# Sums of squares of a hybrid decoder layer as two rounded products, with their low parts on GpSimd

## The reference

```python
def _rms_norm(x, g, eps):
    y = xf * lax.rsqrt(jnp.mean(xf * xf, axis=-1, keepdims=True) + eps)
    return (y * g.astype(jnp.float32)).astype(x.dtype)

q = _rms_norm(q.reshape(b, s, ATTN_HEADS, 2, ATTN_HEAD_DIM), q_g, RMS_EPS) * (ATTN_HEAD_DIM ** -0.5)
k = _rms_norm(k.reshape(b, s, ATTN_HEADS, 2, ATTN_HEAD_DIM), k_g, RMS_EPS)
...
o = _rms_norm(o, sub_g, RMS_EPS) * (1.0 - lambda_init)
```

## Time and profile before

| | us |
|---|---|
| median of 3 runs | 1872.85 (1872.35 to 1877.61) |
| the profiled execution | 1872.82 |
| its span | 1870.8 |
| busy TensorE | 1827.9 |
| busy VectorE | 1133.2 |
| busy ScalarE | 942.4 |
| busy GpSimd | 359.4 |

### The profile page before, as it was taken

How to read it: one execution, slowest core, us unless ns; L and a number is a source line. 1 busy time by engine, 2 the same in 40 slices (tenths; PEclk the granted TensorE clock), 3 DMA queues, 4 the chain that set the end, 5 groups by cost and what they waited for, 6 DMA issues and landing times.

```text
span 1870.8 us, 27353 instructions
## 1 busy us (share of the span) xinstructions
PE 1827.9 (98%) x8653; PEld 1298.2 (69%) x8653; DVE 1133.2 (61%) x1373; ACT 942.4 (50%) x1310; POOL 359.4 (19%) x401
## 2 busy tenths in 40 slices
PE   8999999999999999999999999999999999999997
PEld 6887887887888888887655565566556655665553
DVE  7867867867867333458664565456545654565456
ACT  5676676666667222325454455445544554455441
POOL 1322332332330000013021112111211121112010
PEclk9999999999999999999999999999999999999999
DMA  5232232232241222458999999999999999999998
GB/s 203 86 124 93 80 132 92 78 128 102 79 138 57 94 97 98 162 197 318 421 421 421 421 422 421 422 421 422 421 422 421 421 421 422 421 422 421 422 420 335
DMA packets 95377, 520.06 MB, mean 278 GB/s; under 512 B 13522, under 2 KB 20858, under 8 KB 45032
## 3 DMA queue, kind: packets, MB, share of 16 engines
q1 hardware_dynamic: 87672, 501.08, 67.2%
q0 software_dynamic: 6944, 16.30, 2.2%
q10 hardware_dynamic: 720, 2.16, 0.3%
HBM read 511.52 MB, written 25.51 MB: 287 GB/s over the span
## 4 chain that ended last, share of the span: by engine, by line
PE 81%; DMA 10%; DVE 5%; issue 2%; ACT 1%; DVEq 0%; SPq 0%; ACTq 0%
PE bank L1924 18%; PE bank L1300 15%; PE bank L1682 10%; DMA big<-in_w 10%; PE bank L1955 7%; PE bank L1330 7%; PE bank L1964 6%; PE bank L1729 2%; DVE w_lo L2520 2%; PE bank L1947 2%; PE bank L1375 2%; PE bank L1358 1%; PE bank L1867 1%; DVE x_lo L2532 1%; PE bank L1442 1%
## 5 line engine op out<-in xcount | busy, mean ns | idle before, releaser
L2520 DVE TENSOR_TENSOR w_lo<-big,w_hi 128x2048 fp32r<-128x2048 f32 x141 | 321.9, 2292 | 204.6 <-ACT w_hi L2211 204.6
L2211 ACT ACTIVATE w_hi<-big 128x2048 fp32r<-128x2048 f32 x141 | 268.8, 1918 | 231.1 <-DMA big<-in_w 203.1
L1955 PE MATMUL bank<-big,keep 128*64 128x512 f32 x896 | 203.3, 598 | 0.0
L2520 DVE TENSOR_TENSOR w_lo<-keep,w_hi 128x2048 fp32r<-128x2048 f32 x48 | 109.9, 2292 | 104.0 <-ACT w_hi L2211 103.6
L1300 PE MATMUL bank<-h_hi,wm_hi 128*128 128x512 f32 x408 | 168.8, 414 | 0.0
L1300 PE MATMUL bank<-h_hi,wm_lo 128*128 128x512 f32 x408 | 159.7, 391 | 0.0
L1300 PE MATMUL bank<-h_lo,wm_hi 128*128 128x512 f32 x408 | 159.1, 390 | 0.0
L2211 ACT ACTIVATE w_hi<-keep 128x2048 fp32r<-128x2048 f32 x48 | 92.2, 1921 | 107.3 <-DMA keep<-in_w 97.6
L1955 PEld LDWEIGHTS bank<-big,keep 128*64 128x64 f32 x896 | 59.9, 136 | 117.3 <-issue 117.2
L1924 PE MATMUL bank<-w_hi,x_hi 128*128 128x512 f32 x480 | 134.5, 402 | 3.8 <-DVE w_lo L2520 3.8
L1924 PE MATMUL bank<-w_lo,x_hi 128*128 128x512 f32 x480 | 129.0, 391 | 0.0
(11 more groups left out here) (398 smaller groups left out, 3628.3 us busy)
## 6 DMA issues: line engine op xcount, KB each, us to landing
big<-in_w SPq DMA_DIRECT2D x290, 1024.0 KB, 13.4
keep<-in_w SPq DMA_DIRECT2D x94, 1024.0 KB, 14.2
big<-in_w_mix SPq DMA_DIRECT2D x72, 512.0 KB, 3.3
keep<-in_w_tail SPq DMA_DIRECT2D x44, 512.0 KB, 3.3
keep<-in_x SPq DMA_DIRECT2D x8, 512.0 KB, 4.5
aux<-acum_rows SPq DMA_DIRECT2D x16, 256.0 KB, 3.7
big<-acum_rows SPq DMA_DIRECT2D x16, 256.0 KB, 3.5
keep<-y_tok SPq DMA_DIRECT2D x4, 1024.0 KB, 13.1
```

Source lines behind the costliest of these rows:

```text
L1955: ins = pe.matmul(bank[2 * (c // 2)][r, :], x_s[:, n % 4, CS * (n // 4):CS * (n // 4 + 1)], raw[s][:, c * 512:(c + 1) * 512], start=False, ...
L2211: act.activation(w_hi[:, s], raw[r], ACT.Copy).then_inc(hi_ready, 1)
L2520: dve.tensor_tensor(w_lo[:, s], raw[r], w_hi[:, s].bitcast(F32), ALU.subtract).then_inc(lo_ready, 1)
```

## The change

The three sums of a step become two rounded products each: the block of ones by the high part of the squares (rounded to float32r) and by the low part (square minus high part), added up in PSUM. The ones are copied once to float32r (`block_r`, `ones_r`); for the third sum the stationary operand is one column broadcast to 128.

- ScalarE gets three copies a step: `high_square(0)` and `high_square(1)`, each behind a `take_xb`, and one behind the square of the output. They write to the place of the logits. `make_decay(1)` moves ahead of `root(0)`.
- GpSimd gets three subtractions a step (`low_square`), two behind `make_xs(0)` and one at the end of the step, where the mask of the next step's first chunk moves ahead of it; the mask of its second chunk is behind it. Its last step is written out like those of the other engines.
- TensorE: `project_vz(0)` is cut in three. Its first two blocks of weights run before `y_and_state(0)`; three follow `turn_xb(2)`; then comes `sum_squares(0)`, then the last three, then `sum_squares(1)`. A part of the projection now waits only for the pieces of the value weights that it reads. The third sum moves one quarter of projection 3 further back, and each sum waits for its low part.
- Two semaphores of the routing are taken over from others.

```diff
+        block_r, ones_r = parts("block_r", [P, P], big_base, loop_mem.at + 4 * D), sb("ones_r", [P, 1], F32R)
+        sq_hi, sq_lo = parts("sq_hi", [P, 2, T], aux_base, 0), parts("sq_lo", [P, 2, T], keep_base, 23552 - 3 * KT * P)
...
+                def low_square(i, n, at):
+
+                    pool.wait_ge(sqhi_ready.sem, sqhi_ready.at(i, at))
+                    pool.tensor_tensor(sq_lo[:, n], sq[:, n], sq_hi[:, n].bitcast(F32), ALU.subtract).then_inc(
+                        sqlo_ready.sem, 1)
+
+                def body(i, more):
+                    make_seg(i, 1)
+                    make_xs(i, 0)
+                    low_square(i, 0, 1)
+                    low_square(i, 1, 2)
+                    make_seg(i, 2)
+                    make_xs(i, 1)
+                    make_seg(i, 3)
+                    make_xs(i, 2)
+                    make_xs(i, 3)
+                    if more:
+                        make_seg(i + 1, 0)
+                    low_square(i, 0, 3)
...
+                    def high_square(n):
+
+                        act.wait_ge(proj_read.sem, proj_read.at(i, n + 1))
+                        act.wait_ge(diff_ready.sem, diff_ready.at(i, 0))
+                        act.activation(sq_hi[:, n], sq[:, n], ACT.Copy).then_inc(sqhi_ready.sem, 1)
...
                     squares(0)
                     take_xb(0)
+                    high_square(0)
                     split(i, 7)
                     split(i, 8)
                     squares(1)
                     take_xb(1)
+                    high_square(1)
                     take_xb(2)
+                    make_decay(1)
                     root(0)
-                    make_decay(1)
...
                     act.activation(sq[:, 0], m1_b[:], ACT.Square).then_inc(osq_ready.sem, 1)
+                    act.wait_ge(osq_ready.sem, osq_ready.at(i, 1))
+                    act.activation(sq_hi[:, 0], sq[:, 0], ACT.Copy).then_inc(sqhi_ready.sem, 1)
...
-                    def project_vz(t):
-                        free_proj(i, 6 + t)
-                        pe.wait_ge(plo_ready.sem, plo_ready.at(i, PIECES))
+                    def project_vz(t, k0=0, k1=KT):
+                        if k0 == 0:
+                            free_proj(i, 6 + t)
+                        pe.wait_ge(plo_ready.sem, plo_ready.at(i, 6 + -(-k1 * VZ // D)))
...
-                        pe.matmul(s_b[n][:], block_ones, sq[:, n], start=True, stop=True).then_inc(sums_ready.sem, 1)
+                        pe.wait_ge(sqlo_ready.sem, sqlo_ready.at(i, n + 1))
+                        pe.matmul(s_b[n][:], block_r[:], sq_hi[:, n], start=True, stop=False)
+                        pe.matmul(s_b[n][:], block_r[:], sq_lo[:, n], start=False, stop=True).then_inc(
+                            sums_ready.sem, 1)
...
-                    sum_squares(0)
+                    project_vz(0, 0, KT // 4)
                     y_and_state(0)
                     turn_xb(2)
-                    project_vz(0)
+                    project_vz(0, KT // 4, 5 * KT // 8)
+                    sum_squares(0)
+                    project_vz(0, 5 * KT // 8, KT)
                     sum_squares(1)
...
                     turn_y(2, 8)
+                    project(i + 1, 3, KT // 2, 3 * KT // 4)
                     pe.wait_ge(osq_ready.sem, osq_ready.at(i, 1))
                     pe.wait_ge(logits_ready.sem, logits_ready.at(i, 4))
-                    pe.matmul(s_b[0][:], ones, sq[:, 0], start=True, stop=True).then_inc(osum_ready.sem, 1)
-                    project(i + 1, 3, KT // 2, KT)
+                    pe.wait_ge(sqlo_ready.sem, sqlo_ready.at(i, 3))
+                    pe.matmul(s_b[0][:], ones_r[:].to_broadcast([P, P]), sq_hi[:, 0], start=True, stop=False)
+                    pe.matmul(s_b[0][:], ones_r[:].to_broadcast([P, P]), sq_lo[:, 0], start=False, stop=True).then_inc(
+                        osum_ready.sem, 1)
+                    project(i + 1, 3, 3 * KT // 4, KT)
```

More of the change, by code:

```diff
@@ L633, in _ @@
             def _(pool):
[L634 removed]
+                prime(pool, seg_ready, sqlo_ready, xs_ready, gidx_ready, sidx_ready, pickb_ready, picks_ready, *spare_used[0:2])
                 pool.wait_ge(decays_ready, 3)
[L636 to L672 removed]
@@ new lines, in heads, with make_seg @@
+                def heads(table, i, u):
+                    return table[:, u, bass.ds(i * HPG, HPG)]
+                def make_seg(i, u):
+                    pool.wait_ge(rows_in[u % 2].sem, rows_in[u % 2].at(i, u // 2 + 1))
+                    of = seg_of[u % 2].rearrange("p k (h c) -> p k h c", h=2)
+                    at = heads(a_all, i, u).rearrange("p (k h) -> p k h", k=2)
+                    pool.tensor_tensor(of, of, at.unsqueeze(3).to_broadcast([P, 2, 2, P]), ALU.subtract).then_inc(
+                        seg_ready.sem, 1)
+                    pool.wait_ge(seg_ready.sem, seg_ready.at(i, 2 * u + 1))
+                    pool.tensor_tensor(of, of, tri.unsqueeze(1).unsqueeze(1).to_broadcast([P, 2, 2, P]), ALU.mult).then_inc(
+                        seg_ready.sem, 1)
@@ new lines, in make_xs @@
+                def make_xs(i, u):
+                    pool.wait_ge(m0_read.sem, m0_read.at(i, u + 1))
+                    pool.wait_ge(m1_ready.sem, m1_ready.at(i, min(2 * u, 6)))
+                    pool.wait_ge(ydiag_ready.sem, ydiag_ready.at(i, u))
+                    pool.wait_ge(y_read.sem, y_read.at(i, u))
+                    xv = xb[:, u, 0:GW].rearrange("p (h c) -> p h c", h=HPG)
+                    for dst, src in ((xdt, heads(dtv, i, u)), (xw, heads(wend, i, u))):
+                        pool.tensor_tensor(dst.rearrange("p (h c) -> p h c", h=HPG), xv,
+                                           bcast_inner(src, HD), ALU.mult)
+                    dsk = SMALL["d_skip"][0]
+                    pool.tensor_tensor(xd.rearrange("p (h c) -> p h c", h=HPG), xv,
+                                       bcast_inner(smalls[:, bass.ds(i * HPG + dsk, HPG)], HD),
+                                       ALU.mult).then_inc(xs_ready.sem, 1)
@@ L674, in _ @@
+                make_seg(0, 0)
+                pool.tensor_copy(block_r[:], block_ones)
+                pool.tensor_copy(ones_r[:], ones[:, 0:1])
+                steps_of_mixer(pool, body)
             @block.scalar
             def _(act):
-                prime(act, sigz_ready, phi_ready, ghi_ready, sigm_ready, mhi_ready, taps_ready, silu_ready, proj_read, root_ready, m0_read, decay_ready, exp_ready, yn_ready,
+                prime(act, sigz_ready, sqhi_ready, phi_ready, ghi_ready, sigm_ready, mhi_ready, taps_ready, silu_ready, proj_read, root_ready, m0_read, decay_ready, exp_ready, yn_ready,
@@ L1323, in body @@
                 def body(i, more):
-                    def project_vz(t):
-                        free_proj(i, 6 + t)
-                        pe.wait_ge(plo_ready.sem, plo_ready.at(i, PIECES))
+                    def project_vz(t, k0=0, k1=KT):
+                        if k0 == 0:
+                            free_proj(i, 6 + t)
+                        pe.wait_ge(plo_ready.sem, plo_ready.at(i, 6 + -(-k1 * VZ // D)))
                         hi, lo = (w[:].rearrange("p (a b) -> p a b", a=KT) for w in (vz_hi, vz_lo))
-                        for k in range(KT):
+                        for k in range(k0, k1):
                             for h, w in ((h_hi, hi), (h_hi, lo), (h_lo, hi)):
@@ L1332, in project_vz @@
                                                 stop=(k == KT - 1 and h is h_lo))
-                        ins.then_inc(proj_done.sem, 1)
+                        if k1 == KT:
+                            ins.then_inc(proj_done.sem, 1)
                     def turn_xb(u):
@@ L2095, in head_ov @@
                     for t in range(NT):
-                        pe.wait_ge(ovhot_ready, t + 1)
+                        pe.wait_ge(ovhot_ready.sem, ovhot_ready.at(t + 1))
                         for k in range(TOPK):
@@ L2746, in head_ov @@
                         dve.tensor_tensor(ovid_hot, ovid_hot, bcast_inner(entry1[:, n], NOV + 1), ALU.mult).then_inc(
-                            ovhot_ready, 1)
+                            ovhot_ready.sem, 1)
                     dve.wait_ge(ovtable_ready, 1)
```

39 lines of the change are left out of this document (4 added, 35 removed).

## The result

| | before | after |
|---|---|---|
| median, us (runs) | 1873.88 (7) | 1880.46 (7) |
| lowest to highest | 1872.35 to 1877.61 | 1878.88 to 1881.72 |
| span of the profiled execution | 1870.8 | 1878.5 |
| busy VectorE / ScalarE / GpSimd | 1133.2 / 942.4 / 359.4 | 1122.3 / 953.8 / 398.4 |
| mean mixer step (first C·B product to the next step's, seven steps) | 68.65 | 69.48 |

A forecast was written before the change was run, and what follows sets the result against it. TensorE, with its waits, was taken to bound the mixer step. Eight steps at 0.5 us gave +4.0, less 0.6 for the third sums: +3.4 us on 1872.85, so 1876.3; range 1868 to 1884.

The forecast's parts named there:

- What bounds the kernel: Mixer step of 68.7 us: TensorE busy all the time; a step is its queue plus what it waits for.
- The products' price: TensorE's sums: two rounded products 0.45 us against 0.86, 0.09 a type change; nominally 1.08 us saved a step.
- The third sum gives nothing: Start of step: TensorE's 0.35 us goes to waiting for ScalarE's last SiLU; gain 0.04 a step, 0.6 us together.
- The first sum is later: TensorE reaches the first sum 4.36 us later; ScalarE's root(0) 1.90 later, VectorE's norm_qk(0) at 334.33 instead of 332.43.
- scores(0) waits for norm_qk(1): TensorE's scores(0), held by VectorE's norm_qk(1), starts at 340.75, 0.4 us later than before.
- VectorE's lateness behind it: Behind scores(0): VectorE 0.9 us late, TensorE 0.4; 0.48 slack at third chunk's differences, another 0.1 charged.
- It catches up at the end of the step: VectorE waits there for ScalarE's taps, so none of its lateness is carried into the next step.
- GpSimd gets the port first: Rival, 0.27: chunk 2's mask precedes norm_qk(0) at the shared port; 0.9 to 1.2 us a step, 1881.
- the full saving: Rival, 0.10: neither the SiLU nor norm_qk(1) holds TensorE; 8.6 us saved, 1864.
- norm_qk(1) was late in every step: Answers the rival, 0.15, that VectorE's norm_qk(1) is not late: TensorE keeps 0.34 + 0.04 a step, 1869.5.
- the products are no cheaper: Last rival, 0.03: a broadcast or type change costs 0.4; 1 us a step more than the forecast's sum, 1884.
- the likeliest case: The forecast itself, chance 0.45: +3.4 us to 1876.3, own range 1873 to 1880.

The follow-up runs named there:

- all_seven: Changed kernel with first sum, last SiLU, root(0) and split copy earlier, third sum one block later than before, not two, masks of chunks 2 and 3 later: 1864.24 us.
- places_alone: Changed kernel's new places of the three sums, but one plain f32 product each, without copies and low parts: 1888.41 us, 1.0076 to before.
- both_masks_behind: Changed kernel with GpSimd's masks of chunk 2 and chunk 3 behind make_xs(1) and make_xs(2): 1881.39 us, 1.0044 to before.
- split_ahead: Changed kernel with ScalarE's high part of the next step's second weight split ahead of the norm of y of chunk 0: 1876.81 us, 1.0016 to before.

## Why the prediction was right and wrong

- **What bounds the kernel**: right. The difference is made in the mixer, by TensorE's waits; the gates start 7.2 us later than before (597.55 and 590.35) and the span is 7.7 longer.
- **The products' price**: right. Two rounded products take 0.46 (335.59, 335.82 and one more distance), the third sum with its broadcast column 0.46 (317.18, 317.41, next 317.64). By stretches of a step (mean of seven, us):

| from | before | after | all_seven |
|---|---|---|---|
| first C·B product to the transposes of chunk 1 | 5.82 | 5.81 | 5.72 |
| to the transposes of chunk 3, past both sums | 7.89 | 7.09 | 7.37 |
| to the second chunk's C·B product | 0.33 | 0.83 | 0.33 |
| to scores(0) | 4.51 | 5.16 | 4.49 |
| to the fourth chunk's differences | 32.04 | 32.63 | 32.04 |
| to the next step's first transposes, past the third sum | 17.63 | 17.28 | 17.30 |
| to its first C·B product | 0.44 | 0.68 | 0.33 |

  The first two sums save 0.80 (0.73 worked out) and the third 0.35 (0.35), 1.15 together (1.08). The price of a change of type was read too high: the row of 335.84 has two 128x128 products (x2) and not one, which leaves about 0.05 a change, and the cut of the projection adds two changes and not one. The two slips work against each other.
- **The third sum gives nothing**: right. C·B comes 5.36 after the tap (5.37 forecast) and 0.69 after the transposes (0.8); the low part was done at 316.40 and wanted at 317.18. TensorE reaches the next step's transposes 0.35 earlier and then waits 0.24 longer for the SiLU. From the fourth chunk's differences to the next step 0.12 us is gained, 0.04 was forecast.
- **The first sum is later**: right. Counted from the C·B product ScalarE's Ln is 1.83 later (1.90 on the clock, 1.94 so counted), waiting 1.01 for the sum with the copies and the decay done; VectorE's wait for the root is 38.0 us in eight steps, 4.75 each (about 5). VectorE's wait for the second C·B product is gone, and TensorE waits for next_state(0) instead.
- **scores(0) waits for norm_qk(1)**: right. It starts 0.05 after that instruction's end (344.20), 0.53 later in its step than before (0.44 so counted), 0.34 in the mean of the eight steps. In four of them VectorE needs 5.17 from norm_qk(0) to norm_qk(1), in the step shown 5.46; 5.25 was forecast.
- **VectorE's lateness behind it**: this is the step that failed. The forecast had VectorE 0.9 us late (1.01 in the step shown, 0.88 in the mean), gave 0.48 of slack at the third chunk's differences, and charged "another 0.1". The slack was read from one reader out of several. The one at the fourth chunk, 34 us behind norm_qk(1), had 0.07 us. So the whole lateness was paid. Behind scores(0) TensorE lost 0.63 us a step (32.67 against 32.04) where 0.1 was forecast, and in all the first part of a step grew by 0.97 (51.55 against 50.58) where 0.54 was forecast (0.5, and 0.04 because the C·B product that it is counted from comes earlier). The difference of 0.43 in eight steps is 3.4 us; the change of the medians, 6.6, is 3.2 above the forecast's 3.4. (The median after, 1880.46, is 4.2 above 1876.3, since the kernel before was itself 1.0 slower in these runs than in the three that the forecast started from.)
- **It catches up at the end of the step**: right; steps do not get longer from one to the next.
- **GpSimd gets the port first** (0.27): in one step of eight. In the third the mask and norm_qk(0) met:

```profile
198.03 1.62 DVE L1092 SCALAR_TENSOR_TENSOR big<-big,smalls,keep 128x512 f32<-128x512 f32 x1 [4.88 <-ACT keep L823]
```
```profile
198.06 1.04 POOL L648 TENSOR_TENSOR aux<-aux,a_all 128x512 f32<-128x512 f32 x1 [2.53 <-DMA aux<-acum_rows]
```
```profile
200.04 0.49 PE L1402 MATMUL bank<-big 128*128 128x128 f32 x2 [1.08 <-DVE keep L1140]
```

  So the third step took 70.29, 0.95 above the mean of the others; the rival had it 0.4 to 0.7 above the forecast's step. It is 1 us of the 6.6. The result lies between the forecast and this rival, but the rival's mechanism has little part in it. The range held in part by luck: its upper end, 1884, was there for this rival and the last one, and what used it up was the slack at the fourth chunk, which no rival named.
- **The other rivals**: the full saving did not come, since TensorE waits in four places of a step (for the SiLU, next_state(0), norm_qk(1) and take_y); norm_qk(1) was late in every step; places_alone rules out that the products are no cheaper.
- **The chances**: 1880.46 is inside the range, and half a microsecond above the likeliest case's own range. With 0.35% it is just slower by over 0.3%, where "same" was given more.

## What to carry over

Slack of an engine that falls behind is the smallest over all its later readers until it catches up, not that at the next one: follow its queue to the first long wait, and look at each place where the bounding engine takes something from it. If a queue has no break for 25 us, its length is fixed, and what opens it is as good as on the critical path; a collision moved along it cost the same in both places tried here. Put a faster instruction where its result is not later than before: here a step got 1.08 us shorter, but only with the sum, the SiLU, the mask and the copy each moved to where the next engine's run does not start late.

## What the runs showed of the hardware

- The listed start doesn't say who holds the port. VectorE's norm_qk(0) is listed 0.03 us ahead of GpSimd's mask (198.03 and 198.06) and is the one that was held: 1.62 us in place of 0.75, while the mask took its usual 1.04. The Trainium skill (SBUF — State Buffer, "Who interferes with whom") says that the order of issue decides who blocks, and for the whole instruction; the length of the hold agrees, but the order can't be read from rows that stand so close. In the last step the mask is listed 0.06 us behind norm_qk(0) (546.06 and 546.00) and there the mask is the one held, 1.59 us.
- An instruction with one input in SBUF is held too: the TENSOR_SCALAR on 2 columns took 0.86 us in place of 0.17 in both_masks_behind. The same section counts tensor_scalar among the operations that can take the shared pair; this row agrees.
- GpSimd is held in turn: the mask's two instructions take 1.04 and 1.29 us at their usual, 2.02 (both_masks_behind) and 2.15 (the kernel after, at 339.72) beside VectorE's splits.
- A group of products behind a wait costs some 0.14 us more by itself: y products follow scores(0) after 0.56 us when scores(0) had waited 0.2 us or more, after 0.42 when less or not at all, in all kernels, save where the y products themselves wait for GpSimd. It was in no term of the forecast. In the kernel after it is hidden in the wait for the differences; in split_ahead, where that wait is gone, it is what is left of it (32.16 against 32.04).
